# Pooling spread between the u tiles, and router logits with the activations stationary, in a decoder layer on one core

## The reference, cut to what matters

```python
h = rmsnorm(x, g_mix); proj = h @ w_in               # 1024 -> [u 512 | v 512 | z 512]
ua = jax.nn.gelu(proj[..., :2 * WIDTH_A])
u = ua[..., :WIDTH_A];  v = rmsnorm(ua[..., WIDTH_A:], g_v);  z = proj[..., 2 * WIDTH_A:]
a_out = u * (tril(w_s) @ v + b_s)                    # per head, in chunks of 128 tokens
for g, w in enumerate((2, 4, 8, 16)):                # pooling, 128 channels per group
    pooled_g = (sum of the last w rows of z_g) / min(w, pos + 1) - z_g
    b_out_g = (pooled_g @ w_pool[g]) * s_pool_g
x = x + concatenate([a_out, b_out]) @ w_out
...
g_logits = t @ w_group + b_group                     # 4 columns
e_logits = t @ w_router + b_router                   # 16 columns
```

## Time and profile before

| | us |
|---|---|
| median of 3 runs | 1089.63 (1085.09 to 1090.03) |
| the profiled execution | 1089.73 |
| its span | 1087.9 |
| TensorE busy | 931.1 (86%) |
| VectorE busy | 462.5 (43%) |
| ScalarE busy | 405.0 (37%) |
| mean granted TensorE clock | 0.938 of 2.4 GHz |

### The profile page before, as it was taken

The page is one execution under the profiler, slowest core; times in us unless marked ns, Lnnn a source line. Parts: engine busy times, 40 slices in busy tenths (PEclk is TensorE's granted clock), DMA queues, the critical chain, the costliest instruction groups (busy, mean ns, idle before and its releaser), DMA issues. The chain is left out here.

```text
span 1087.9 us, 13921 instructions
## 1 busy us (share of the span) xinstructions
PE 931.1 (86%) x4691; PEld 758.8 (70%) x4691; DVE 462.5 (43%) x625; ACT 405.0 (37%) x656; POOL 158.5 (15%) x192
## 2 busy tenths in 40 slices
PE   4999968999999987899999999844999999898940
PEld 3779847778865766587888887633787787776830
DVE  3341193432113446572322222446564556675314
ACT  5442201410014657552211111612465556665313
POOL 3210000000010110000000000402023332323315
PEclk9989988999999989999999999975999999999975
DMA  7312020180015794620000000862789898989548
GB/s 237 136 39 73 20 84 20 74 332 1 1 55 205 284 339 139 237 81 6 1 1 1 1 1 1 344 256 90 233 251 274 263 287 251 337 290 292 105 106 331
DMA packets 40844, 165.24 MB, mean 152 GB/s; under 512 B 4987, under 2 KB 5387, under 8 KB 32058
## 3 DMA queue, kind: packets, MB, share of 16 engines
q1 hardware_dynamic: 28738, 112.74, 28.3%
q0 software_dynamic: 11456, 49.45, 16.1%
q10 hardware_dynamic: 576, 2.10, 0.5%
HBM read 133.04 MB, written 31.34 MB: 151 GB/s over the span
## 5 line engine op out<-in xcount | busy, mean ns | idle before, releaser
L1790 DVE TENSOR_TENSOR e_Wl<-raw,e_Wh x48 | 109.9, 2292 | 83.6 <-ACT e_Wh L1735 83.3
L529 PE MATMUL ps<-a_wh,a_hTh 128*128 128x512 f32 x288 | 116.3, 404 | 2.6 <-DVE a_hTl L487 1.3
L1735 ACT CAST e_Wh<-raw x48 | 91.6, 1909 | 67.0 <-issue 58.8
L531 PE MATMUL ps<-a_wl,a_hTh 128*128 128x512 f32 x288 | 114.1, 396 | 0.0
L530 PE MATMUL ps<-a_wh,a_hTl 128*128 128x512 f32 x288 | 114.1, 396 | 0.0
L1617 PE MATMUL ps<-e_Wh,e_xTh 128*128 x224 | 91.7, 409 | 0.0
L1618 PE MATMUL ps<-e_Wl,e_xTh 128*128 x224 | 89.0, 397 | 0.0
L1619 PE MATMUL ps<-e_Wh,e_xTl 128*128 x224 | 88.6, 396 | 0.0
L1704 POOL DMA_INDIRECT x_rows<-e_y,dst x27 | 51.3, 1899 | 200.0 <-DMA x_rows<-e_y,dst 125.0
L529 PEld LDWEIGHTS ps<-a_wh,a_hTh 128*128 128x128 f32 x288 | 55.7, 193 | 14.4 <-DVE a_wl L367 1.6
L531 PEld LDWEIGHTS ps<-a_wl,a_hTh 128*128 128x128 f32 x288 | 55.2, 192 | 11.9
(11 more groups left out here) (309 smaller groups left out, 1869.9 us busy)
## 6 DMA issues: line engine op xcount, KB each, us to landing
raw<-in_w_e SPq DMA_DIRECT2D x48, 1024.0 KB
t_raw<-in_w_att SPq DMA_DIRECT2D x64, 256.0 KB, 4.2
a_raw<-in_w_mix SPq DMA_DIRECT2D x20, 512.0 KB, 6.1
t_ring<-in_kc POOLq DMA_DIRECT2D x8, 1024.0 KB, 6.4
t_ring<-in_vc POOLq DMA_DIRECT2D x8, 1024.0 KB, 8.7
x_rows<-x SPq DMA_DIRECT2D x10, 512.0 KB, 4.9
a_xin<-in_x SPq DMA_DIRECT2D x9, 512.0 KB, 5.1
x<-in_x SPq DMA_DIRECT2D x9, 512.0 KB, 6.0
```

The costliest lines, as they stand in the source:

```text
L529: pe.matmul(out, hTh[:, c, own], h, start=(c == 0), stop=False)
L531: last = pe.matmul(out, hTh[:, c, own], l, start=False, stop=(c == KC - 1))
L1735: act.copy(Wh[:, ds(off + q * PIECE, PIECE)], raw[:, ds(off + q * PIECE, PIECE)]).then_inc(hi_ok[q], 1)
L1790: dve.tensor_tensor(Wl[:, at], raw[:, at], Wh[:, at].bitcast(F32), ALU.subtract).then_inc(lo_ok[q], 1)
```

## The change

Mixing: `pool_group` is split. `pool_sums(g, lo, hi)` makes doublings lo to hi - 1 of group g, `pool_means(g)` the rest. `pool_part(t)` stands at the end of VectorE's step for u tile t: sums of group 0, 1, 2 and 3 in tiles 0, 1, 3 and 5 to 6, means and the sample part in tiles 0, 2, 4 and 7. The sums that are computed are the same ones.

Routing: the operands of the logits product change places. hT is stationary (128 columns), the weights move (20 columns), so the result has tokens on the partitions at once; lgT, its copy and its turning back are gone. The bias is no product any more: it is loaded on all partitions and added by VectorE where it copied.

```diff
-            def pool_group(g):
+            def pool_sums(g, lo, hi):
+                E = 16 + SEQ
+                for n in range(lo, hi):
+                    src, k, dst = z[:, g, :] if n == 0 else (s0, s1)[(n - 1) % 2][:, :], 1 << n, (s0, s1)[n % 2][:, :]
+                    then_sum(dve.tensor_tensor(dst[:, 2 * k - 1:E], src[:, 2 * k - 1:E], src[:, k - 1:E - k], ALU.add))
+
+            def pool_means(g):
                 w = WINDOWS[g]
                 E = 16 + SEQ
-                src, k, other = z[:, g, :], 1, (s0, s1)
-                for n in range(g + 1):
-                    dst = other[n % 2][:, :]
-                    then_sum(dve.tensor_tensor(dst[:, 2 * k - 1:E], src[:, 2 * k - 1:E], src[:, k - 1:E - k], ALU.add))
-                    src, k = dst, 2 * k
-                dst = other[(g + 1) % 2][:, :]
+                src, dst = (s0, s1)[g % 2][:, :], (s0, s1)[(g + 1) % 2][:, :]
...
-            dve.wait_ge(cv_st, 16 * 2)
-            for g in range(NG):
-                dve.wait_ge(z_ok, 3 * g + 3)
-                if g:
-                    dve.wait_ge(pool_ok, g)
-                pool_group(g)
-                pool_sample(g)
+            SLOTS = {0: ((0, 0, 1),), 1: ((1, 0, 2),), 3: ((2, 0, 3),), 5: ((3, 0, 2),), 6: ((3, 2, 4),)}
+            ENDS = {0: 0, 2: 1, 4: 2, 7: 3}
+            def pool_part(t):
+                for g, lo, hi in SLOTS.get(t, ()):
+                    if g == 0:
+                        dve.wait_ge(cv_st, 16 * 2)
+                    elif lo == 0:
+                        dve.wait_ge(pool_ok, g)
+                    dve.wait_ge(z_ok, 3 * g + 3)
+                    pool_sums(g, lo, hi)
+                if t in ENDS:
+                    pool_means(ENDS[t])
+                    pool_sample(ENDS[t])
...
+                pool_part(t)
...
-            def copy_logits(n):
-                act.wait_ge(lg_ps, n + 1)
-                act.copy(lgT[:, n, :], ps[0:NL2, 2 + n % 3, 0:P]).then_inc(lgT_ok, 1)
...
             def logits(n):
                 pe.wait_ge(hT_ok, n + 1)
-                if n >= 3:
-                    pe.wait_ge(lgT_ok, n - 2)
-                out = ps[0:NL2, 2 + n % 3, 0:P]
                 for c in range(KC):
-                    pe.matmul(out, wr[:, c, :], hT[n % 2][:, c, :], start=(c == 0), stop=False)
-                pe.matmul(out, brow[:, :], ones[0:1, :], start=False, stop=True).then_inc(lg_ps, 1)
-
-            def turn_logits(n):
-                pe.wait_ge(lgT_ok, n + 1)
-                pe.transpose(ps[:, 5, n * NL2:(n + 1) * NL2], lgT[:, n, :], ident[0:NL2, 0:NL2]).then_inc(lgt_ps, 1)
+                    last = pe.matmul(ps[:, 5, n * NL2:(n + 1) * NL2], hT[n % 2][:, c, :], wr[:, c, :], start=(c == 0),
+                                     stop=(c == KC - 1), skip_group_check=True)
+                last.then_inc(lg_ps, 1)
...
-            dve.wait_ge(lgt_ps, NT)
+            dve.wait_ge(lg_ps, NT)
+            bias = brow[:, :].rearrange("p (o n) -> p o n", o=1).to_broadcast([P, NT, NL2])
             lg = ps[:, 5, 0:NT * NL2].rearrange("p (t n) -> p t n", n=NL2)
-            dve.tensor_copy(EL[:, :, :, :].rearrange("p t g e -> p t (g e)"), lg[:, :, EG:NL2])
-            then(dve.tensor_copy(GL[:, :, :], lg[:, :, 0:EG]))
+            v(EL[:, :, :, :].rearrange("p t g e -> p t (g e)"), lg[:, :, EG:NL2], bias[:, :, EG:NL2], ALU.add)
+            then(v(GL[:, :, :], lg[:, :, 0:EG], bias[:, :, 0:EG], ALU.add))
```

More of the change, by code:

```diff
@@ L1309, in routing_buffers @@
     sb("wr", [P, KC, NL2])
-    sb("brow", [1, NL2])
+    sb("brow", [P, NL2])
     sb("before", [P, P])
@@ L1318, in load_routing_buffers @@
     consts = [(keep["gffn"][:, :], io["g_ffn"].to_broadcast([P, D])), (keep["wr"][:, :, :], io["w_r"]),
-              (keep["brow"][:, :], io["b_r"]), (keep["before"][:, :], io["before"]),
+              (keep["brow"][:, :], io["b_r"].to_broadcast([P, NL2])), (keep["before"][:, :], io["before"]),
               (keep["cst"][:, :], io["cst"].to_broadcast([P, 4 + NT + NTILE + P])), (keep["tok"][:, :, :], io["tok"])]
@@ L1370, in routing_block @@
         ones_ok, h_st, x2_st = sem("ones_ok"), sem("h_st", XB), sem("x2_st")
-        sq_ok, r_ok, xs_ok, tr_ps, hT_ok, lg_ps, lg_ok = (
-            sem(n) for n in ("sq_ok", "r_ok", "xs_ok", "tr_ps", "hT_ok", "lg_ps", "lg_ok"))
+        sq_ok, r_ok, xs_ok, tr_ps, hT_ok, lg_ps = (
+            sem(n) for n in ("sq_ok", "r_ok", "xs_ok", "tr_ps", "hT_ok", "lg_ps"))
         step_ok, gd_ok, ge_ok, dm_ok, ex_ok, M_ok, cnt_ps, AB_ok, idx_ps = (
             sem(n) for n in ("step_ok", "gd_ok", "ge_ok", "dm_ok", "ex_ok", "M_ok", "cnt_ps", "AB_ok", "idx_ps"))
-        lgT_ok, lgt_ps = sem("lgT_ok"), sem("lgt_ps")
-        lgT = sb("lgT", [NL2, NT, P])
         fall4 = cst[:, 0:4]
@@ L1427, in _ @@
                 act.copy(hT[n % 2][:, :, :], ps[:, BT(n), :].rearrange("p b (c t) -> p (b c) t", t=P)).then_inc(hT_ok, 1)
[L1428 to L1431, removed]
             act.wait_ge(gd_ok, 1)
@@ L1464, in _ @@
                     logits(n - 1)
-                if n >= 3:
-                    turn_logits(n - 3)
             logits(NT - 1)
-            for n in range(NT - 3, NT):
-                turn_logits(n)
             pe.wait_ge(M_ok, 1)
```

## The result

| | before | after |
|---|---|---|
| median | 1090.16 (1085.09 to 1096.52, 12 runs) | 1081.99 (1077.90 to 1092.13, 12 runs) |
| the profiled execution | 1089.73 | 1082.33 |
| mean granted TensorE clock | 0.938 | 0.926 |

The ratio of the mean times is 0.9935, with a 95% interval of 0.9907 to 0.9963: 0.65% faster, some 7 us, where 20 were forecast. It is the case of rival E, "about 1082": the clock was full for a part of the routing loop and half for the rest.

The account below looks back on a forecast made before the run. TensorE carries the 1087.9 us span, losing time idle before a(0) in mixing and as routing's tile-by-tile chain. 1089.7 - 15.5 (mixing) - 4.3 (routing) = 1069.9, forecast 1070; own range 1067 to 1073, with rivals 1063 to 1093.

Parts of the forecast that it names:

- rival E: Routing loop: clock full for part and half for the rest, between A and rival C, about 1082; chance 0.12.
- 13.34 + 2.20 = 15.5 us: Mixing: TensorE's hole before a(0) goes, 13.34; a(0) to a(1) shrinks from 8.14 to 5.94, returning 2.20.
- the fullest slot: Mixing, VectorE's tile 3: 6.4 us of work against 5.94, making a(4) 0.5 us late at most, covered.
- rival D: Mixing: VectorE's slots overflow, tile 3's 0.5 us repeated in five tiles, 2.7 returned, total 1072.6; chance 0.06.
- Price of a record: Routing logits: 0.105 us per record at full clock, the 128-column load setting the spacing; sixteen are 1.68.
- the additive reading: Routing logits: 64 moving columns cost 0.058 and the load 0.047, so 20 columns make 0.065 a record.
- rival B: Routing: cheap loads, 0.065 a record, a tile 2.3, 9.7 us won, total 1064.5; chance 0.10.
- With 0.105 a tile is 1.02 + 1.88 = 2.90: Routing loop at full clock: transposes 1.02 plus logits 1.88 per tile, against 3.36 before.
- rival C: Routing loop at half clock: 0.215 a record, a tile 5.36, 16.7 us lost, total 1090.9; chance 0.34.
- The routing term: Routing: tile 8's logits end at 713.7, so VectorE begins on them 4.3 us earlier than 718.01.
- A: The main forecast: routing at full clock, 0.105 us a record, total 1070; chance 0.38.
- The other half of the reasoning: Routing, second argument against rival C: the transposes already stood ahead of the clock's rise in the earlier kernel.

## Why the prediction was right and where it was wrong

**Mixing: right.** 13.34 + 2.20 = 15.5 us was forecast and 15.52 measured, and 14 us between the medians with this part alone. That the start of the program, which spreads (the first gelu starts at 144.83 to 147.91 in the eleven traces), was alike in the pair of traces is luck; counted from that gelu the gain is 15.57. The forecast named the fullest slot and its lateness of 0.5 us, and 171.64 shows it late by 0.47; no other slot overflowed, so rival D has nothing in the trace.

**Price of a record: right at full clock.** 0.105 was forecast and 0.106 measured; with 20, 32 and 56 moving columns the tile is the same 2.61 or 2.62, so the additive reading of the earlier trace rows, on which rival B stood, is refuted. That the load sets the spacing is the reading left over; a load's own row, 190 ns at full clock, is longer than that spacing. A tile was forecast at 2.90: I had put 0.2 us on the boundary and carried the old 1.02 for the transposes, but measured are 1.70 and 0.91. That small term was on the safe side; at full clock the routing change with 56 columns gives 32.04 - 26.03 = 6.0 us, where I had 4.3.

The Trainium skill, "TensorE: Matmul & The Clock Gate", section "LDWEIGHTS (loading the stationary operand)", has a load's time as its columns divided by 1.2 in ns, which makes an estimate of 107 ns for 128 columns. The spacing of 0.106 us at full clock agrees with it; the loads' own rows, 190 ns there and 333 ns at half clock, do not, nor does the spacing of 0.204 at half clock, and the measurements decide.

**The failed step.** It is "With 0.105 a tile is 1.02 + 1.88 = 2.90", applied to all tiles, that is, the choice of a loop at full clock throughout over rivals C and E. Two sets of logits and most of the third ran so, the other six at 5.01 us a tile. With a record at 0.204 instead of C's 0.215 the half-clock tile was cheaper than the 5.36 given, too. (C's own sum ends at 725.5 + 1.72 + 2 x 3.64 = 734.5 and not at 734.7; nothing hangs on the difference.) The routing term was forecast at -4.3 and measured at +7.37, an error of 11.7 us; with attention's +1.8 and the -1.0 at the end, neither of them forecast, 1069.9 becomes 1082.3, the time of the profiled execution. So that rival E's 1082 was met to 0.3 us is partly luck: it was put between A and C with a half-clock tile that was too dear, and two unforecast differences came on top.

A sign for it had been in the rows: the earlier trace rows held a stretch of the same loads under 64 moving columns, busy for 7.94 of 7.95 us and at 0.50 throughout. Rival C named it, and my "against" was that "the loop never idles". It never did: it was busy for 29.10 of 29.10 us at a clock of 0.50. So a busy TensorE is no ground for a full clock; for 29.00 of these 29.10 us a load was running. But the stretch in the earlier trace rows shows another thing than the loop. It starts at half clock behind a long wait, and does not rise:

```profile
741.55 7.94 PE L1476 MATMUL ps<-r_A,r_big 128*128 128x64 f32 x36 [13.65 <-DVE r_A L1584]
```

The loop starts high and falls, and there 56 or 32 columns, fewer than these 64, were enough to keep the clock, beside the transposes of each tile. What raises the clock and what keeps it are two questions, and one does not answer the other. The other half of the reasoning held: in the nine traces whose loop starts at half clock, the clock rose between 0.3 us ahead of the first logits and 0.7 us into them, behind or at the end of sixteen transposes (in the other two it was full already), and so rival C, half clock from the start, was seen in none.

The same page, section "HAM oscillation — how this bites in real kernels", tells of a clock that falls when TensorE waits for data between its matmuls. By that rule this loop, without a wait, would have kept the full clock; the trace disagrees, with a fall to 0.50 in a stretch of 29.10 us that is all busy. In section "Part 4: PE-mode transpose" the page says that the full clock does not engage for transposes; no run here bears that out, since in nine traces sixteen transposes behind 4.64 us of idle end in the rise just named.

**Open.** Why single executions of the changed kernel spread by 10 us and more, and what the late executions of the kernels with 32 columns and with the unread matmul did. Nor did any run move few columns under narrow loads, so whether the full loads have a part in the fall, or only the few moved columns, is not shown.

## What to carry to other kernels

Where a narrow f32 product is TensorE's only work, price it at both clocks before you choose the stationary operand: with 128 stationary columns a record stood 0.106 us from the next at full clock whether 20 or 56 columns moved, and the loop took 26 us where the clock held and 39 where it fell. Up to the 56 columns tried, moving more was free; padding 20 columns to 56 turned a loss of 7.4 us into a gain of 6, and held the clock in eleven executions of eleven, where 32 columns had one late execution in six. And work that fills a queue ahead of the first thing TensorE wants belongs behind it, in slots whose fullest is added up row by row: that part of the sum was right to a tenth of a microsecond, counted from the start of the stretch that was changed.

## What the runs showed of the hardware

The clock can fall while TensorE is busy without a gap: 1.00 to 0.50 some 7 us into 20-column logits with full loads, in four traces of four (two of the changed kernel, one of its routing part alone, one with four wide matmuls ahead of the loop). It stayed full in all traces in which more was moved, under the same loads (32 or 56 columns) or between them (one matmul of 256 columns per tile). It was not raised in 7.94 us of such loads under 64 columns that began at 0.50, and it rose at the end of sixteen transposes or within 0.7 us behind them, in the nine traces whose loop began at 0.50. The loads themselves follow the clock: 190 ns and 0.106 us of spacing at 1.00, 333 ns and 0.204 at 0.50. And adding work that nobody reads to a saturated engine made the kernel 11 to 15 us faster than the changed one (medians of 1068.48 to 1070.69 against 1081.99 and 1083.06).
